# Forget-gate stage of a three-layer block rewritten: heads in pairs, fused mask and maximum, head norms as rows

## What is computed

```python
h = concat([meta_tokens (16), x (256)])            # 272 positions
n1 = rmsnorm(h, norm1_w)
q, k, v, fg, u = split(n1 @ w_in)                  # 8 heads of width 64; u has 512 columns
q = rmsnorm(q per head, q_norm_w); k = rmsnorm(k per head, k_norm_w)
cum_logf = cumsum(log_sigmoid(fg + b_fgate))       # per head, over positions
a_out = causal softmax(q k^T / 8 + cum_logf[t] - cum_logf[s]) v
pooled = trailing means of u over 2, 4, 8, 16 positions, minus u, by 4 groups of 128 columns
p_out = (pooled @ w_pool) * pool_scale
h = h + concat([a_out, p_out]) @ w_out
h = h + (silu(n2 @ w_gate) * (n2 @ w_up)) @ w_down # n2 = rmsnorm(h, norm2_w)
return h[16:]
```

## Time and profile before

| | us |
|---|---|
| median of 3 runs (lowest, highest) | 1073.36 (1072.41, 1076.38) |
| the profiled execution | 1071.25 |
| its span, first to last instruction | 1069.9 |
| TensorE busy, share of the span | 1022.6 (96%) |
| VectorE, ScalarE, GpSimd busy | 678.9, 511.7, 28.0 |
| forget-gate stage from the end of Cq1 to the end of the first unit of f2 | 717.4 to 884.6 |

### The profile page before, as it was taken

The page is one execution under the profiler, slowest core; times in us unless marked ns, Lnnn a source line. Parts: engine busy times, 40 slices in busy tenths (PEclk is TensorE's granted clock), DMA queues, the critical chain, the costliest instruction groups (busy, mean ns, idle before and its releaser), DMA issues.

```text
span 1069.9 us, 18810 instructions
## 1 busy us (share of the span) xinstructions
PE 1022.6 (96%) x7935; PEld 967.7 (90%) x7935; DVE 678.9 (63%) x1198; ACT 511.7 (48%) x885; POOL 28.0 (3%) x30
## 2 busy tenths in 40 slices
PE   6999999999999999799899999999978999999998
PEld 5998989999999988668899999999945599999998
DVE  4778847876767877674586767675333357565564
ACT  5555435654545647563465545462212345444442
POOL 0000000000000000000000000000201000000000
PEclk9999999999999999699999999999866599999999
DMA  9433324455464454101544454542310034555541
GB/s 354 178 138 119 121 77 167 178 213 200 160 226 164 148 214 179 61 1 40 231 193 180 176 197 157 215 179 83 116 40 0 7 137 173 200 194 197 174 182 41
DMA packets 24564, 160.74 MB, mean 150 GB/s; under 512 B 2848, under 2 KB 4640, under 8 KB 5792
## 3 DMA queue, kind: packets, MB, share of 16 engines
q1 hardware_dynamic: 23904, 159.27, 40.6%
q10 hardware_dynamic: 576, 0.26, 0.1%
HBM read 158.21 MB, written 1.05 MB: 149 GB/s over the span
## 4 chain that ended last, share of the span: by engine, by line
PE 84%; DVE 9%; ACT 4%; DMA 2%; issue 1%; SPq 0%; DVEq 0%
PE ps L352 81%; DVE wl L1025 3%; PE ps L361 2%; DMA raw<-in_w 2%; ACT wh L1722 1%; DVE col L1034 1%; DVE arena L1268 0%; ACT arena L1976 0%; DVE arena L1043 0%; DVE arena L1256 0%; DVE arena L1059 0%; DVE xt L1111 0%; ACT arena L1857 0%; ACT arena L1855 0%; ACT arena L1972 0%
## 5 line engine op out<-in xcount | busy, mean ns | idle before, releaser
L1025 DVE TENSOR_TENSOR wl<-raw,wh 128x1024 fp32r<-128x1024 f32 x292 | 342.1, 1221 | 153.7 <-ACT wh L1722 153.6
L352 PE MATMUL ps<-xh,wh 128*128 128x256 f32 (+1 forms) x1312 | 374.5, 285 | 12.5 <-DVE wl L1025 9.1
L352 PE MATMUL ps<-xl,wh 128*128 128x256 f32 (+1 forms) x1312 | 370.5, 282 | 0.0
L352 PE MATMUL ps<-xh,wl 128*128 128x256 f32 (+1 forms) x1312 | 370.0, 282 | 0.0
L1722 ACT CAST wh<-raw 128x1024 fp32r<-128x1024 f32 x292 | 290.1, 1046 | 160.6 <-PE ps L352 129.6
L352 PEld LDWEIGHTS ps<-xh,wh 128*128 128x128 f32 x1312 | 250.9, 191 | 13.9 <-DVE wl L1025 9.1
L352 PEld LDWEIGHTS ps<-xl,wh 128*128 128x128 f32 x1312 | 250.9, 191 | 0.1
L352 PEld LDWEIGHTS ps<-xh,wl 128*128 128x128 f32 x1312 | 250.8, 191 | 0.0
L352 PE MATMUL ps<-fh,wh 128*128 128x256 f32 x528 | 149.4, 283 | 0.0
L352 PE MATMUL ps<-fh,wl 128*128 128x256 f32 x528 | 149.4, 283 | 0.0
L352 PE MATMUL ps<-fl,wh 128*128 128x256 f32 x528 | 149.4, 283 | 0.0
(11 more groups left out here) (203 smaller groups left out, 1113.9 us busy)
## 6 DMA issues: line engine op xcount, KB each, us to landing
raw<-in_w SPq DMA_DIRECT2D x145, 1024.0 KB, 4.8
raw<-in_w SPq DMA_DIRECT2D x2, 512.0 KB, 6.1
arena<-in_mem SPq DMA_DIRECT2D x1, 1024.0 KB, 12.8
out<-xt SPq DMA_DIRECT2D x8, 128.0 KB, 2.0
small<-in_small SPq DMA_DIRECT2D x1, 943.5 KB, 9.0
arena<-in_sel SPq DMA_DIRECT2D x1, 768.0 KB, 4.4
xt<-in_x SPq DMA_DIRECT2D x2, 256.0 KB, 4.3
xt<-in_x SPq DMA_DIRECT2D x1, 512.0 KB, 6.3
```

The lines of the kernel that those rows point to most:

```text
L352: return pe.matmul(out, lhsT, rhs, start=start, stop=stop, skip_group_check=True)
L1025: v.tensor_tensor(L[:, s], src[:, s], f32(H[:, s]), ALU.subtract).then_inc(*w_lo.up(2 * i + a))
```

## The change

It touches the forget-gate stage of all engines' programs, and some constants that all stages use.

- **Order.** TensorE: Cq0, Cq1, Ck0, sums_C, Ck1, spread_C, forget, Cv0, head_sums q and k, forget_t, Cv1, head_scale q (2 banks, two products each) and k (4), decay, spread_r1, Cu0, then the heads. Banks are given out by hand. ScalarE squares x between the casts after Cq0 and those after Cq1. The scaling of x with g_final (L1559 before) comes after the heads' loop has nearly ended.
- **Head norms as rows.** `hsel`, 128 x 32 with 1/64, is the stationary operand: 4 + 4 products of 256 and 272 columns give the mean squares as 8 rows. VectorE adds epsilon in place of the squares, GpSimd raises 8x256 (q) and 8x272 (k) to the power -0.5, and `head_scale` reads them. `head_rows` and its copies are gone.
- **Heads in pairs.** One turn takes the two heads of a pair, on partitions 0-63 and 64-127, their products set alternately. Scores have one bank for each half (6, 7), the turned probabilities banks 4 and 5; the 16 meta columns of the second block are turned into the upper half of the output bank (3).
- **Fused mask and maximum.** `tensor_tensor_reduce` adds the mask and takes the minimum of the negated sum in one instruction; the exponential has scale -1.
- **Dense units between heads.** Cu1 after the first pair's scores; chunks 4, 5 of Co0 and Co1 in turn 2, chunks 6, 7 in turn 4, half of Co2 after it. The last chunks of Co0, Co1, Co2 come together, then Co3. Casts and rests there run 3 units ahead.
- **Constants.** `ones` and `halves` go; the factor 1/1024 or 1/128 lies in the column `inv` and in `gw`, so that variances need only an added epsilon.

```diff
         unit_f("Cq0", 0, XH, XL, x_c)
         unit_f("Cq1", 1, XH, XL, x_c)
+        unit_wide("Ck0", banks_of(2, 3), x_c)
...
-        unit_wide("Ck0", bank_a, x_c)
+        unit_wide("Ck1", banks_of(5, 6), x_c)
         spread("spread_C", 7, rst_, TTM)
...
+        def head_sums(tag, sq4, w, k0, bank):
+                last = mm(P[0:8, 0:w], cn("hsel", j * 8, j * 8 + 8), v3(sq4[:, 0:4 * w], w)[:, j, :], j == 0, j == 3)
+        def head_scale(name, bank, blocks, sq4, w, row):
+            t.wait_ge(*row)
...
+            for n, j in enumerate(blocks):
+                last = mm(P[:, n * w:(n + 1) * w], selc[0:8, 1024 + j * 128:1024 + (j + 1) * 128], sq4[0:8, 0:w], True, True)
...
+        unit_t("Cv1", banks_of(3, 5), XFH, XFL, x_c, meta_last)
+        for j in range(2):
+            head_scale(f"hscale_q{j}", j, (2 * j, 2 * j + 1), sqh, T, s_pow.at(POW["q"]))
+        for j, b in enumerate((2, 4, 6, 7)):
+            head_scale(f"hscale_k{j}", b, (j,), kn_sq, TM, s_pow.at(POW["k"]))
...
+        def c_scores(j):
+            for i, (o, w) in enumerate(((272, 144), (0, 272))):
+                for g in range(2):
+                    r = g * 64
+                    mm(P[g][:, o:o + w], cq[r:r + 64, j, i * 128:(i + 1) * 128], ck[r:r + 64, j, 0:w], True, False)
+                for g in range(2):
+                    r, h = g * 64, 2 * j + g
+                    last = mm(P[g][:, o:o + w], selc[r:r + 64, h * 128:(h + 1) * 128], cT[r:r + 64, 0:w], False, True)
...
+        for k in range(6):
+            if k < 4:
+                c_scores(k)
+            if k == 0:
+                unit_wide("Cu1", banks_of(2, 0), x_c)
+            if k == 1:
+                pool_out(0, 1)
+                pool_out(1, 1)
+            if k == 2:
+                out_part("Co0", banks_of(0), (4, 5), out_c)
+                out_part("Co1", banks_of(1), (4, 5), out_c)
+            if 2 <= k:
+                c_out(k - 2)
+            if k == 3:
+                pool_out(2, 2)
+                pool_out(3, 2)
+            if k == 4:
+                out_part("Co0", None, (6, 7), out_c)
+                out_part("Co1", None, (6, 7), out_c)
+            if 1 <= k < 5:
+                c_turn(k - 1)
+            if k == 4:
+                out_part("Co2", banks_of(2), KOUT[0:4], out_c)
...
+                v.tensor_tensor_reduce(EE[:, 0:272], P[:, 0:272], m2, -1.0, 3.0e38, ALU.add, ALU.min, st[:, 0:1])
+                v.tensor_tensor_reduce(EE[:, 272:416], P[:, 272:416], m2[:, 128:272], -1.0, 3.0e38, ALU.add, ALU.min,
+                                       st[:, 1:2]).then_inc(*ps.freed(name))
...
         for j in range(4):
-            if j >= 2:
-                rests(f"Co{j}", 2)
+            rests(f"Co{j}", 3)
             residual(f"Co{j}", j, "f2", "n2")
...
-        for n in range(2):
-            power(f"q{n}", hs[:, 24 + n * 8:32 + n * 8], hs[:, n * 8:n * 8 + 8],
-                  c_hv.at(0) if n == 0 else ps.done("hsum_q"))
-        for n, m in enumerate((128, 128, NM)):
-            power(f"k{n}", hs[0:m, 184 + n * 8:192 + n * 8], hs[0:m, 160 + n * 8:168 + n * 8],
-                  c_hv.at(1 + n) if n < 2 else ps.done("hsum_k"))
+        power("q", sqh[0:8, 0:T], sqh[0:8, 0:T], ps.done("hsum_q"))
+        power("k", kn_sq[0:8, 0:TM], kn_sq[0:8, 0:TM], ps.done("hsum_k"))
```

More of the change, by code:

```diff
@@ L48 @@
 CONST = [
[L49 to L50 removed]
+    ("ident", 128), ("tri", 128), ("trim", TM), ("mask2", TM), ("hsel", 32),
+    ("valid", 2), ("one", 1), ("inv", 2), ("mhalf", 1),
 ]
@@ L858, in pe_program @@
         last.then_inc(*ps.full("sums_C"))
-        unit_wide("Ck0", bank_a, x_c)
+        unit_wide("Ck1", banks_of(5, 6), x_c)
         t.wait_ge(*c_r1.at(0))
[L861 to L865, removed]
+        spread("spread_C", 7, rst_, TTM)
+        P = ps.open("forget", 4)
+        t.wait_ge(*ps.vacant("forget"))
+        for c in range(8):
+            s = 320 + c * 8
+            last = mm3(P[0:8, 0:TM], smh[:, s:s + 8], sml[:, s:s + 8], XFH(c), XFL(c), c == 0, c == 7)
+        last.then_inc(*ps.full("forget"))
+        def head_sums(tag, sq4, w, k0, bank):
             name = "hsum_" + tag
@@ L893, in pe_program @@
[L893 to L902, removed]
@@ L909, in pe_program @@
         last.then_inc(*ps.full("forget_t"))
[L910 to L918, removed]
+        unit_t("Cv1", banks_of(3, 5), XFH, XFL, x_c, meta_last)
[3 more added lines that the diff above has]
+            head_scale(f"hscale_k{j}", b, (j,), kn_sq, TM, s_pow.at(POW["k"]))
+        P = ps.open("decay", 3)
         t.wait_ge(*ps.vacant("decay"))
         t.wait_ge(*sp_c.at(1))
-        two = cst[:, CN["tri"][0]:CN["tri"][0] + 256]
         lf = hs[:, 120:144]
@@ L1549, in wide @@
             v.tensor_tensor(dst, ps[name][:, 0:TM], rs_[:, :], ALU.mult).then_inc(*ps.freed(name))
-        wide("Ck0.0", ck[:, 0, :])
-        wide("Ck0.1", ck[:, 1, :])
+        for j in range(4):
+            wide(f"Ck{j // 2}.{j % 2}", ck[:, j, :])
         rests("Ck1", 2)
-        wide("Ck1.0", ck[:, 2, :])
-        wide("Ck1.1", ck[:, 3, :])
-        d.wait_ge(*ps.done("spread_r1"))
-        for c in range(8):
-            d.wait_ge(*c_sq.at(c))
-            last = v.scalar_tensor_tensor(xs[c], xs[c], sm("gfin", c, c + 1), r1b, ALU.mult, ALU.mult)
-        last.then_inc(*c_x.up(0))
+        d.wait_ge(*ps.ready("forget"))
+        v.tensor_copy(cT[0:8, :], ps["forget"][0:8, 0:TM]).then_inc(*ps.freed("forget"))
         def value_c(j):
@@ L1628, in dve_program @@
         last.then_inc(*ps.freed("decay"))
+        take("spread_r1", r1b, T)
+        rests("Cu0", 2)
         def pool_u(g):
@@ L1673, in dve_program @@
         pool_u(0)
         pool_u(1)
-        for k in range(14):
-            if k >= 6 and k % 2 == 0:
-                pair_low(f"co{(k - 6) // 2}", (k - 6) // 2, c_hi)
-            if k < 8:
-                c_scores(k)
-            if 1 <= k < 9:
+        for k in range(6):
+            if k == 2:
+                pool_low(0)
+                pool_low(1)
+            if k < 4:
+                c_scores(k)
+            if k == 0:
+                rests("Cu1", 2)
+                pool_u(2)
+                pool_diff(0)
+                pool_u(3)
+                pool_diff(1)
+            if 1 <= k < 5:
@@ L1697, in dve_program @@
                 pool_low(2)
-            if k == 6:
                 pool_low(3)
-            if k == 9:
-                rests("Co0", 1)
-            if k == 10:
-                rests("Co1", 1)
+            if k >= 2:
+                pair_low(f"co{k - 2}", k - 2, c_hi)
+            if k == 4:
+                for c in range(8):
+                    d.wait_ge(*c_sq.at(c))
+                    last = v.scalar_tensor_tensor(xs[c], xs[c], sm("gfin", c, c + 1), r1b, ALU.mult, ALU.mult)
+                last.then_inc(*c_x.up(0))
```

460 lines of the change are left out of this document (202 added, 258 removed).

## The result

The changed kernel takes 1108.29 us (median of 4 runs, 1104.06 to 1112.76), the kernel before 1072.88 beside it: ratio 1.0327, 95% interval 1.0278 to 1.0377. It is slower by some 35 us. The profiled execution took 1107.75 us, its span is 1106.3.

What follows compares the result with a forecast made beforehand. TensorE's own stream was taken as the bound (84% of the chain of waits). Heads starting at 854.8 plus 66.5 put f2u0's end at 921.3 against 884.6: 36.7 us more, 1108, by the median 1110; range 1029 to 1130.

Steps and rivals of the forecast that it cites:

- the opposite sign: Whole kernel: the change makes it faster, chance 0.27; the range was drawn down to 1029 to reach the hidden-power case.
- Before Cv1's end: TensorE from Cq1's end at 717.4: 44.3 us to Cv1's end at 761.7, against 766.1 before, Cv1 at clock 1.00.
- The power: GpSimd's powers on rows: 0.157 us per column plus 0.38 fixed, q 40.6 and k 43.1 us, TensorE waiting until 837.0.
- The 2 us: Added to GpSimd's two powers for VectorE's weight splits that fall in; bounds 0 and 4.7.
- the rival "hidden": GpSimd's powers cost less per column in long rows and end before Cv1: 40 us gained, 1033; chance 0.22.
- From the power to the heads: TensorE after k's power: hscale_k 3.7, decay 4.7, spread_r1 0.8, Cu0 6.05 + 2.6; 17.8 us, heads at 854.8.
- The pair loop: First scores to Co3's end, at full clock: 53.8 us instead of 96.4; a pair's scores 1.6, output product 1.4.
- the 4.4 us: Pair loop: added to the sum if a pair's output products on column halves take 2.5 us instead of 1.4.
- the lower bound: VectorE's fused mask and maximum: 0.57 us per head's step at the rates of the two additions; upper bound 1.13.
- The rival "heads gain less": Pair loop: serial halves +6, the loop at 1.2 GHz up to +15, giving 1115 to 1125; chance 0.20, inside slower.
- The end of the stage: After Co0: four residual cycles of 4.6 us delay f2's input; f2u0 ends at 65.0, not 59.5, plus 1.5 for clock.
- the forecast's 36.7: Total lengthening in us: end of f2's first unit at 921.3 against 884.6, added to the kernel's time.

Runs made afterwards that it cites:

- experiment 2: Changed kernel, with GpSimd's power taken of only 64 of q's 256 columns and 136 of k's 272, the others left as variances: 1049.0 us (one run).
- experiment 3: Changed kernel, with GpSimd multiplying q's and k's rows by the constant instead of raising them to the power: 1035.18 us, 0.9646 of the kernel before.
- experiment 5: Changed kernel, with score and output products of a pair set one head after the other instead of alternately: 1112.29 us, 1.0393 of the kernel before.
- experiment 6: Changed kernel, with two additions and two reductions per head in place of the fused mask and maximum: 1111.91 us, 1.0387 of the kernel before.
- experiment 7: Changed kernel, with the weight split two units ahead instead of three at the residuals of Co1 to Co3: 1101.44 us, 1.0282 of the kernel before.
- experiment 9: Changed kernel with experiment 7's edit, rows kept, ScalarE's square root and VectorE's reciprocal replacing GpSimd's power: 1028.65 us, 0.9620 of the kernel before.
- experiment 1: Changed kernel, with the head norms of the kernel before (tokens x heads, three powers, turned into rows): 1030.74 us, 0.9595 of the kernel before.

## Why the prediction was right, point by point

It gave 1110 us, a range of 1029 to 1130 that took in the opposite sign, and a chance of 0.71 for slower; 1108.29 was measured. The mechanism is the one it named: two powers of some 40 us each, for which TensorE waits, against a loop some 40 us shorter. By its own steps:

- **Before Cv1's end.** From the start of the sums to Cv1's end it had 38.2 us, the trace 38.0; Ck1's clock fell, Cv1 stayed at 1.00, head sums took 3.7. Right.
- **The power.** 40.6 and 43.1 us, with 2 more for VectorE's splits, 85.7 in all; measured 41.1 and 43.7, 84.8. The slope taken from 2 and 8 columns, 0.157, holds to 272 with 0.159 to 0.161. The 2 us were wrong in kind: four halves of splits run beside q's power and none beside k's, in the changed kernel and in experiment 2, and q's two lengths give 0.306 us and 0.1594 per column where k's two give 0.385 and 0.1592, so the splits added nothing. The slightly larger slope made 1.1 us of it up. That the slope can't be carried from a short to a long row was the argument for the rival "hidden"; experiments 2 and 3 close it. The Trainium skill (GPSIMD Engine Reference, section 3.1) has some 2.6 cycles per element for a two-input operation; the multiplication of 256 columns in 0.60 us agrees with it (the forecast's estimate by it was 0.55), the power at 41.1 does not.
- **From the power to the heads.** 17.8 us forecast, 15.8 measured (837.4 to 853.2): Cu0 took 6.8 us, not 8.65, since the clock rose within its first 1.1 us.
- **The pair loop.** 53.8 us forecast, 55.3 measured, at clock 1.00 as assumed. Scores of a pair 1.6 against 1.68, output product 1.4 against 1.45. The column halves, of which no row of before showed an overlap, do overlap: 1.45 alternately, 2.81 one after the other (experiment 5), so the 4.4 us that serial products would have added did not come. The Trainium skill (TensorE: Matmul & The Clock Gate, Part 3, packing small matmuls) says this of column tiles, and here the runs agree. The fused step costs 0.44 and 0.30 us, the lower bound. Taken back alone, the alternation is worth 6.7 and the fused step 6.8 of the 41.2 us by which the loop shrank; the rest, the new order with its dense units at clock 1.00 where before had 0.50 for most of the loop, was not taken apart.
- **The rival "heads gain less".** Its two prices were +6 for serial halves (experiment 5: 6.7) and up to +15 for the lower clock. It was not what happened, but it was closer than the forecast made it look: with 0.7 us more of VectorE's work for each head the clock came down twice and the loop took 6.8 us more (experiment 6).
- **The end of the stage.** It had two waits on the last input chunks from a residual cycle of 4.6 us. There are two, 1.9 and 2.9 us, the cycle is 4.61, and experiment 7 takes one of them away by moving the split. f2's first unit ended at 919.3, forecast 921.3; the clock fell as allowed for, but in the second unit (919.3 to 922.7).

Over the stage: 69.3 us more before the heads (134.4 from Cq1's end to the first scores, 65.1 before), 41.2 fewer in the loop, 6.8 more behind it: 34.9 of the 36.4 us by which the span grew. Another 1.4 stand before the stage, within what profiles of one code differ by there.

That the forecast's 36.7 lies within half a microsecond of the span's growth is in part luck. From Cq1's end to the end of f2's first unit it had 203.9 us and the trace has 200.5: the power took 0.9 less, the steps up to the heads 2.0 less, the end of the stage 1.9 less, the loop 1.5 more. Most of these 3.4 us came back through the clock's fall behind that unit, some 1.7 (half of 3.4 at half clock), and through the 1.4 ahead of the stage.

## What to carry to other kernels

Before moving an elementwise step to another layout, ask what its engine pays for: here GpSimd's power paid for columns and not for partitions, so the same 4224 roots cost 7.3 us on 128 partitions (16 for the last eight columns) and 84.8 on 8, while ScalarE and VectorE did the rows in 5.6. A slope and an intercept from two short shapes in the trace were enough here to forecast a row thirty times longer within 2%, though no row before showed that the line would hold, and a rival built as a kernel (a multiplication in the power's place) told operation from layout in one run. A large gain and a larger loss can lie in one edit: take the parts one at a time; with the old head norms the other parts make this kernel 4% faster than before.

## What the runs showed that had not been expected

- A power on GpSimd has the same duration, within a nanosecond, in five programs (41115 or 41116, and 43685 ns), while its additions of 128x265 in the pair loop took 1136 ns on the mean (626 in the kernel before) and those of 128x271 652.
- Products of two heads on row halves overlap even where they only meet: 2.27 us for 16 passes in head order, 1.68 alternately, 3.3 if nothing overlapped (twice 1.67). On column halves head order gives 2.81, twice a single head's, and alternation 1.45.
- TensorE's clock fell to 1.2 GHz at 762.9 in experiment 9 with no wait of more than 0.3 us in the 35 us ahead of it, during products with 8 rows that kept the engine busy, and it fell in experiment 6 after a wait of 3.1 us but not in the changed kernel after one of 1.4. In experiment 1 it did fall (794.6 to 798.0) soon after a wait of the same 1.4, and the loop took 55.4 us all the same: the later wait of 1.4 that the changed kernel has there (for VectorE's L1623) was gone. Why one of two like stretches keeps the clock stays open.
